# A decoder layer on one core: the FFN down projection with tokens as output rows instead of output columns

## The reference

```python
def conv_ffn(x, prev, up, cw, cb, down):
    a = x @ up
    gate, val = jnp.split(a, 2, axis=-1)
    gc, new = causal_conv(gate, prev, cw)
    h = jax.nn.gelu(gc + cb, approximate=True) * val
    return h @ down, new
...
    f, new_ffn = conv_ffn(rmsnorm(x, g_ffn_pre), ffn_prev, ffn_up, ffn_conv_w, ffn_conv_b, ffn_down)
    x = x + rmsnorm(f, g_ffn_post)
```

## Time and profile before

| | us |
|---|---|
| median of 3 runs (1368.5, 1371.78, 1371.96) | 1371.78 |
| profiled execution, span from first to last instruction | 1368.2 |
| median less span | 3.6 |
| TensorE busy (matmuls / weight loads) | 1335.9 / 1324.1 |
| VectorE, ScalarE, GpSimd busy | 759.0, 505.5, 115.1 |

### The profile page before, as it was taken

How to read it: one execution, slowest core, us unless ns; L and a number is a source line. 1 busy time by engine, 2 the same in 40 slices (tenths; PEclk the granted TensorE clock), 3 DMA queues, 4 the chain that set the end, 5 groups by cost and what they waited for, 6 DMA issues and landing times.

```text
span 1368.2 us, 24903 instructions
## 1 busy us (share of the span) xinstructions
PE 1335.9 (98%) x9043; PEld 1324.1 (97%) x9043; DVE 759.0 (55%) x1153; ACT 505.5 (37%) x731; POOL 115.1 (8%) x224
## 2 busy tenths in 40 slices
PE   6999999999989999999999999999999999999996
PEld 5999999999978999999999999999999999999995
DVE  7457755544468655544655554455554456555544
ACT  4333333333454333333333333333332333333653
POOL 4551000000034000000000000000000000000001
PEclk9999999999989999999999999999999999999998
DMA  8655455555534555456545545645545565454543
GB/s 249 162 142 135 118 147 144 150 154 149 146 110 109 143 148 153 126 149 183 143 137 154 143 128 149 190 131 157 145 134 142 152 169 157 135 154 124 138 130 97
DMA packets 383104, 199.30 MB, mean 146 GB/s; under 512 B 3924, under 2 KB 380224, under 8 KB 383064
## 3 DMA queue, kind: packets, MB, share of 16 engines
q1 hardware_dynamic: 382992, 198.56, 52.9%
q0 software_dynamic: 80, 0.31, 0.1%
HBM read 195.42 MB, written 3.56 MB: 145 GB/s over the span
## 4 chain that ended last, share of the span: by engine, by line
PE 94%; DVE 2%; SPq 2%; POOL 1%; DMA 1%; issue 0%; ACT 0%; DVEq 0%; ACTq 0%
PE mm L438 30%; PE mm L442 30%; PE mm L439 30%; POOL xT L1438 1%; DMA raw<-in_w_in_dram 1%; SPq L309 1%; PE tb L688 1%; DVE y_tok L1340 1%; DVE w_lo L948 1%; PE tb L480 0%; PE tb L438 0%; DVE sq L1227 0%; PE tb L439 0%; PE tb L442 0%; SPq L323 0%
## 5 line engine op out<-in xcount | busy, mean ns | idle before, releaser
L438 PE MATMUL mm<-a_hi,w_hi 128*128 128x320 f32 x1888 | 588.3, 312 | 0.4 <-DVE w_lo L948 0.4
L442 PE MATMUL mm<-a_lo,w_hi 128*128 128x320 f32 x1888 | 586.2, 310 | 1.9 <-DVE a_lo L1003 1.8
L439 PE MATMUL mm<-a_hi,w_lo 128*128 128x320 f32 x1888 | 585.3, 310 | 0.0
L718 ACT ACTIVATE w_hi<-raw 128x1024 fp32r (+3 forms) x404 | 370.7, 966 | 456.4 <-PE mm L442 444.9
L948 DVE TENSOR_TENSOR w_lo<-raw,w_hi 128x1024 fp32r<-128x1024 f32 (+1 forms) x404 | 441.8, 1135 | 133.3 <-ACT w_hi L718 133.3
L442 PEld LDWEIGHTS mm<-a_lo,w_hi 128*128 128x128 f32 x1888 | 355.3, 188 | 3.7 <-DVE a_lo L1003 3.6
L438 PEld LDWEIGHTS mm<-a_hi,w_hi 128*128 128x128 f32 x1888 | 355.3, 188 | 1.7 <-DVE w_lo L948 0.7
L439 PEld LDWEIGHTS mm<-a_hi,w_lo 128*128 128x128 f32 x1888 | 355.3, 188 | 0.3
L438 PE MATMUL mm<-m_hi,w_hi 128*128 128x320 f32 x960 | 299.2, 312 | 0.0
L442 PE MATMUL mm<-m_lo,w_hi 128*128 128x320 f32 x960 | 297.3, 310 | 0.0
L439 PE MATMUL mm<-m_hi,w_lo 128*128 128x320 f32 x960 | 297.3, 310 | 0.0
(11 more groups left out here) (184 smaller groups left out, 666.5 us busy)
## 6 DMA issues: line engine op xcount, KB each, us to landing
raw<-in_ffn_up_dram SPq DMA_DIRECT2D x88, 1024.0 KB, 5.7
raw<-in_ffn_down_dram SPq DMA_DIRECT2D x64, 704.0 KB, 4.8
raw<-in_w_in_dram SPq DMA_DIRECT2D x34, 1024.0 KB, 5.6
raw<-in_w_out_dram SPq DMA_DIRECT2D x16, 1024.0 KB, 6.0
x_tok<-in_x_prompt_dram SPq DMA_DIRECT2D x4, 512.0 KB, 6.9
out_dram<-y_tok SPq DMA_DIRECT2D x8, 256.0 KB
x_tok<-in_x_sample_dram SPq DMA_DIRECT2D x4, 128.0 KB, 6.8
out_dram<-y_tok SPq DMA_DIRECT2D x4, 128.0 KB
```

Of the source, the lines that this page charges most:

```text
L438: pe.matmul(out, w_hi[:, s], tile(hi, k), start=start, stop=False)
L439: pe.matmul(out, w_lo[:, s], tile(hi, k), start=False, stop=False)
L442: return pe.matmul(out, w_hi[:, s], tile(lo, k), start=False, stop=stop)
L718: act.activation(w_hi[:, d:d + half], src, ACT.Copy).then_inc(w_hi_done, 1)
```

## The change

The down projection of each group is computed the other way round: a block of `h` (128 inner channels, up to 128 tokens) is the stationary operand and 512 columns of `ffn_down` move past it, so that a result has tokens as rows and 512 output channels along the free side.

- **Pieces.** A group has 4 column quarters `n`, each in three weight pieces `j` of 4, 4 and 3 inner blocks (`PARTS`), 12 pieces in all (`N_PIECES`), each 512 columns wide. Per inner block and quarter TensorE does `down_row` for the three token tiles in the order `D_TILES` = (2, 0, 1): three matmuls for each full tile, two for the sample tile. For the samples `h_hi` holds the 64 rounded columns and beside them the 64 columns of what is left, so one 128-wide stationary operand does both with w_hi, the result's halves being added up at the end; w_lo takes a stationary operand of 64 columns. That is 8 matmuls of 512 columns where before there were 4 x 3 = 12 of 320, and 4 x 4 x 11 x 8 = 1408 in all.
- **Banks.** The sums are in the six `tb` banks, three for each of two quarters in turn. VectorE adds them to `f_tok` (`add_rows`, `sum_rows`), which lies where `f` was. The `mm` banks are free for the units.
- **End.** No unit turns `f`, and `token_sums(4)` is gone. ScalarE squares each row piece and sums it along the row in the same instruction (`square_row`). The gain comes as a row spread over the partitions by one transfer from ScalarE's queue; GpSimd multiplies the first three quarters by it, VectorE the last (`gain_last`). In the last group the last two pieces are interleaved by token tile, so that the tiles end one after the other, and each has its own factor. Twelve pieces leave: seven on VectorE (`leave`), five on ScalarE and GpSimd.
- **Elsewhere.** GpSimd's zeroing of `f` is gone, the second part of `h` is made by two VectorE instructions instead of one, and some small regions change place.

```diff
-    PER_GROUP = 2 * NG + KD
+    QD = D // 512
+    PARTS = [(0, 4), (4, 4), (8, NG - 8)]
+    N_PIECES = len(PARTS) * QD
+    PER_GROUP = 2 * NG + N_PIECES
+    D_TILES = (2, 0, 1)
...
+    f_tok = sb("f_tok", [P, QD, 3, 512], where="f")
+    gain = sb("gain", [P, D], where="a_hi", plus=24576)
+    s_low = sb("s_low", [TS, 512], where="a_hi", plus=24576 + 8192)
+    junk = sb("junk", [P, 512], where="acc")
+    h_hi = sb("h_hi", [P, NG, HW], F32R, where="m_hi")
+    h_lo = sb("h_lo", [P, NG, SEQ], F32R, where="m_lo")
+    ssq = sb("ssq", [P, 3, QD])
...
-        UNITS = sorted([(m, "x", m // 3, m % 3) for m in range(3 * (KD // 4))] +
-                       [(4 * k4 + 5 + i, "f", k4, i) for k4 in range(KD // 4 - 1) for i in range(3)] +
-                       [(12, "state", n, 0) for n in range(2)])
-        UNITS += [(KD, "f", KD // 4 - 1, i) for i in range(3)]
-        Y_POOL = [(1, 0), (1, 2), (2, 2)]
-        Y_ORDER = [(k4, i) for k4 in range(QD) for i in range(3) if (k4, i) not in Y_POOL]
+        UNITS = [("x", n // 3, n % 3) for n in range(3 * QD)] + [("state", n, 0) for n in range(2)]
+        UNIT_AT = {6 + n: n for n in range(len(UNITS))}
+        N_UNITS = len(UNITS)
+
+
+        Y_POOL = [(0, 2), (1, 2), (0, 0), (1, 0), (0, 1)]
+        Y_ORDER = [(2, 2), (3, 2), (2, 0), (3, 0), (1, 1), (2, 1), (3, 1)]
 
...
+                for j in range(N_PIECES):
+                    n, (k0, nk) = j // len(PARTS), PARTS[j % len(PARTS)]
+                    load(C_FFN // 2 + g * (PER_GROUP // 2) + NG + j // 2, j % 2,
+                         down[:, bass.ds(g * NG + k0, nk), n * 512:(n + 1) * 512], 4 * nk, 512)
...
+            def down_row(g, e, i, k, slot, start, stop, bank):
+
+                t0, nt = TT[i]
+                o = (e * 4 + slot) * 512
+                whi, wlo = w_hi[:, o:o + 512], w_lo[:, o:o + 512]
+                hi = h_hi[:, k, t0:t0 + nt]
+                if nt == P:
+                    pe.matmul(bank[:, :], hi, whi, start=start, stop=False)
+                    pe.matmul(bank[:, :], hi, wlo, start=False, stop=False)
+                    return pe.matmul(bank[:, :], h_lo[:, k, t0:t0 + nt], whi,
+                                     start=False, stop=stop)
+                both = h_hi[:, k, t0:t0 + 2 * nt]
+                if start:
+                    pe.matmul(bank[:, :], both, whi, start=True, stop=False)
+                    return pe.matmul(bank[0:nt, :], hi, wlo, start=False, stop=stop)
+                pe.matmul(bank[0:nt, :], hi, wlo, start=False, stop=False)
+                return pe.matmul(bank[:, :], both, whi, start=False, stop=stop)
+
...
+            def piece_ready(g, j):
+                pe.wait_ge(w_lo_done, 2 * (C_FFN + g * PER_GROUP + 2 * NG + j) + 2)
+
+            def down_tile(g, j, x):
+
+                n, (k0, nk) = j // len(PARTS), PARTS[j % len(PARTS)]
+                i = D_TILES[x]
+                if k0 == 0:
+                    if type(g) is int and g == GROUPS - 1 and n >= 2:
+                        pe.wait_ge(full_done, 3 * (n - 2) + x + 1)
+                    elif type(g) is not int or 4 * g + n >= 2:
+                        pe.wait_ge(rows_taken, 3 * (QD * g + n - 2) + x + 1)
+                for k in range(k0, k0 + nk):
+                    if n == 0 and x == 0:
+                        ready_h(g, k)
+                    last = down_row(g, j % 2, i, k, k - k0, k == 0, k == NG - 1, tb[3 * (n % 2) + x])
+                return last
+
+            def down_piece(g, j, beside=None):
+                piece_ready(g, j)
+                for x in range(3):
+                    last = down_tile(g, j, x)
+                    if x == 2:
+                        last.then_inc(used, 1)
+                    elif j % len(PARTS) == len(PARTS) - 1:
+                        last.then_inc(rows_done, 1)
+                    if beside and x < 2:
+                        beside(2 * j + x)
+
+            def down_pieces(g):
+                for j in range(N_PIECES):
+                    down_piece(g, j)
...
-            for m in range(KD):
-                mine = [n for n, u in enumerate(UNITS) if u[0] == m]
-                chunk(C_FFN // 2 + g * (PER_GROUP // 2) + NG + m // 2, m % 2, m_hi, m_lo, range(NG),
-                      ready_h(h_hi_done, g), ready_h(h_lo_done, g),
-                      {3 + 2 * x: [lambda n=n: turn_unit(n)] for x, n in enumerate(mine)})
-            token_sums(4)
-            for n, u in enumerate(UNITS):
-                if u[0] == KD:
-                    turn_unit(n)
+            for j in range(N_PIECES - 2):
+                down_piece(g, j, beside)
+            j = N_PIECES - 2
+            piece_ready(g, j)
+            piece_ready(g, j + 1)
+            for x in range(3):
+                down_tile(g, j, x)
+                down_tile(g, j + 1, x).then_inc(used if x == 2 else rows_done, 1)
...
+            def split_piece(g, j):
+
+                blocks = KD if j >= N_PIECES else 4 * PARTS[j % len(PARTS)][1]
+                split_hi(C_FFN // 2 + g * (PER_GROUP // 2) + NG + j // 2, j % 2, blocks)
+
+            def down_splits(g):
+                for j in range(N_PIECES):
+                    split_piece(g, j + 2)
...
+            def square_row(n, x):
+
+                i = D_TILES[x]
+                nt = TT[i][1]
+                act.wait_ge(full_done, 3 * n + x + 1)
+                act.wait_ge(row_squared, 3 * n + x)
+                act.activation(junk[0:nt, :], f_tok[0:nt, n, i, :], ACT.Square,
+                               accum_out=ssq[0:nt, i, n:n + 1]).then_inc(row_squared, 1)
...
+            act.preload_act_table(ACT.Sqrt)
+            for j in range(N_PIECES):
+                for x in range(2):
+                    if 2 * j + x in UNIT_AT:
+                        take_unit(UNIT_AT[2 * j + x])
+                if j < N_PIECES - 2:
+                    split_piece(GROUPS - 1, j + 2)
+                if j == 0:
+                    act.dma_start(gain[:, :], g_ffn_post.to_broadcast([P, D])).then_inc(gain_b_in, 16)
+                if j % len(PARTS) == 0 and j:
+                    for x in range(3):
+                        square_row(j // len(PARTS) - 1, x)
+            for x in range(3):
+                square_row(QD - 1, x)
+                root_of(x)
+                if x == 0:
+                    scale_row(0, 0)
+                    scale_row(0, 1)
+                elif x == 1:
+                    scale_row(1, 2)
+                    scale_row(1, 3)
+            scale_row(2, 4)
...
-                dve.tensor_tensor(tile(m_lo, i), val[:, :], tile(m_hi, i).bitcast(F32),
+                dve.tensor_tensor(h_tile(h_lo, SEQ, i, 0, SEQ), val[:, 0:SEQ],
+                                  h_tile(h_hi, HW, i, 0, SEQ).bitcast(F32), ALU.subtract)
+                dve.tensor_tensor(h_tile(h_hi, HW, i, T, HW), val[:, SEQ:T],
+                                  h_tile(h_hi, HW, i, SEQ, T).bitcast(F32),
                                   ALU.subtract).then_inc(h_lo_done, 1)
...
+            def add_rows(g, n, x):
+
+                i, bank = D_TILES[x], tb[3 * (n % 2) + x]
+                wait_rows(g, n, x)
+                mine = f_tok[:, n, i, :]
+                if type(g) is int and g == 0:
+                    dve.tensor_copy(mine, bank[:, :]).then_inc(rows_taken, 1)
+                else:
+                    dve.tensor_tensor(mine, bank[:, :], mine, ALU.add).then_inc(rows_taken, 1)
...
+            def sum_rows(n, x):
+
+                g, i, bank = GROUPS - 1, D_TILES[x], tb[3 * (n % 2) + x]
+                wait_rows(g, n, x)
+                if i < 2:
+                    mine = f_tok[:, n, i, :]
+                    dve.tensor_tensor(mine, bank[:, :], mine, ALU.add).then_inc(full_done, 1)
                     return
...
+                mine, other = f_tok[0:TS, n, i, :], f_tok[TS:P, n, i, :]
+                dve.tensor_tensor(s_low[:, :], bank[TS:P, :], other, ALU.add).then_inc(halves_made, 1)
+                dve.tensor_tensor(mine, bank[0:TS, :], mine, ALU.add).then_inc(halves_made, 1)
+                dve.wait_ge(halves_made, 2 * n + 2)
+                dve.tensor_tensor(mine, mine, s_low[:, :], ALU.add).then_inc(full_done, 1)
...
+            def gain_last(x):
+
+                i = D_TILES[x]
+                mine = f_tok[0:TT[i][1], QD - 1, i, :]
+                dve.tensor_tensor(mine, mine, gain[0:TT[i][1], (QD - 1) * 512:QD * 512],
+                                  ALU.mult).then_inc(gained_last, 1)
...
+            g = GROUPS - 1
+            step(dve.memset(ssq[:, :, :], 0.0))
+            for j in range(N_PIECES - 1):
+                if j % len(PARTS) == len(PARTS) - 1:
+                    for x in range(3):
+                        sum_rows(j // len(PARTS), x)
+                if j < N_PIECES - 2:
+                    split_piece(g, j + 2)
+            dve.wait_ge(row_squared, 3 * (QD - 1))
+            step(dve.tensor_reduce(rest[:, :], ssq[:, :, 0:QD - 1], mybir.AxisListType.X, ALU.add))
```

(78 more changed lines are left out.)

271 lines of the change are left out of this document (124 added, 147 removed).

## The result

The changed kernel took 1377.25 us (median of 4 runs, 1375.55 to 1379.51) beside 1370.72 us for the kernel before on the same chip (4 runs, 1368.5 to 1371.96). The ratio is 1.0053, 95% interval 1.0039 to 1.0066: half a per cent slower. The forecast was 1376.7 us. One of the later runs, of turn_twice, took 1895.5 us at a mean granted clock of 0.655 and is left out of every comparison.

What follows compares the result with a forecast made beforehand. TensorE was taken as the bound until the end work. Terms 9.4 - 3.9 + 2.9 + 1.0 - 4.5 = +4.9 us gave a 1373.1 us span, plus 3.6 for the median 1376.7 us; range 1358 to 1389.

Steps and rivals of the forecast that it cites:

- Bound by TensorE: Whole span until the end work: only TensorE's time counts, busy 98% of the span, with other engines waiting for it.
- Price of 512 columns: Down matmuls: 226.7 ns each, columns plus a fixed 13.3 ns; 1408 replacing 2112 of 320 columns, +9.4 us.
- Rival D: Sample tile: each of 352 changes between 64 and 128 stationary columns costs 0.07 us, +25 us, 1401; chance 0.04.
- a spread of the sample tile's starts: Down parts: if alternating 64 and 128 stationary columns spreads these starts, the prediction is wrong.
- Rival A: Down matmuls: the remainder hides, 213.3 ns or little more per 512 columns, -13.9 us together, 1358; chance 0.18.
- Rival C: Down matmuls: the remainder grows in proportion to columns, 234.7 ns per 512, +16 us, 1388; chance 0.16.
- Rival E: Between weight pieces elsewhere than the joint: pieces come late, up to 16 x 1 us; chance 0.02.
- Turning: Last down part: 36 transposes of f, at 109 ns each, go, -3.9 us.
- Joining: Last two pieces: joined matmuls wait for a split that starts only when piece 9 is done, +2.9 us.
- Clock: Behind the joint's wait: half clock for 3.41 us may follow, +1.0 us, between 0 and 1.6.
- The end: Behind the last matmul: 13.0 us of end work instead of 17.5, -4.5 us, give or take 1.5.
- The sum: Whole kernel: all terms together +4.9 us, 1373.1 on the profiled span, 1376.7 with 3.6 added for the median.

Runs made afterwards that it cites:

- turn_twice: Changed kernel with the transposes of nine of the twelve xT units made twice, 36 more in the last down part: 1382.31 us, ratio 1.0081.
- all_wide: Changed kernel with the sample tile's w_lo product given 128 stationary columns instead of 64, so none is narrower: 1374.32 us, ratio 1.0034.
- the probe: Separate kernel of float32r matmuls alone, 48 per shape, layer not computed, run once: 146.7 ns at 320 moving columns, 227.5 at 512, with 128 stationary.
- halves: all_wide with each 512-column matmul made as two of 256, 704 in a down part: 1393.63 us, ratio 1.0157.
- own_place: Changed kernel with the last weight piece split into SBUF that xT no longer needs, not into piece 9's place: 1372.99 us, ratio 1.0022.
- apart: Changed kernel with the last two pieces run one after the other instead of joined: 1377.67 us, ratio 1.0052.
- own_wide: Changed kernel with the edits of own_place and all_wide together: 1371.19 us, ratio 1.0008 to the kernel before.

## Why the prediction held, step by step

- **Bound by TensorE: right.** In the middle of the span nothing delays it, before or after, and the terms below that are on its path show in full.
- **Price of 512 columns: the mechanism right, the term mis-sized.** Full-width matmuls cost the 226.7 ns chosen (all_wide's 79.81 us). The term was +9.4 and measured +11.4: 4 x (79.81 - 77.44) = 9.5 for the full-width price, and 4 x 0.49 = 2.0 for the 44 matmuls a part with 64 stationary columns and what they do to their neighbours. Rival D put 0.07 us on each of 352 changes of width, 25 us in all; the 2.0 is the most that can be of its kind, since part of it is the narrow width itself. The prediction's own sign of it, a spread of the sample tile's starts, did come, but small: 231.1 ns on average instead of 226.7., cited against D, have transposes of 128 moving columns; at 320 the probe shows no cost either, only at 512.
- **Rival A fell** (the probe: no shrinking remainder from 256 to 512 columns; halves: a repeated stationary operand pays too), and so did the Trainium skill's page TensorE: Matmul & The Clock Gate (Back-to-back issue gap): 215.8 ns by it, 226.7 measured. (The page gives that gap for an isolated matmul and states a shorter sustained one, about 131 ns at 512 columns; no stretch here averages under 226.7 at 512.) **Rival C fell**: 234.7 by it. **Rival E** did not show: no gap between pieces but the joined one.
- **Turning: right**, -3.9 forecast. turn_twice puts 36 back for 3.85; by the ledger 3.5 came off. The difference of 0.4 is spread over the 14 units left, 0.03 us each, an estimate from 6.44 us for 55 transposes.
- **Joining: right.** +2.9 forecast, +3.1 measured, by own_place due to the shared place. The forecast took the joint as given; it did not ask what the joint buys. apart shows 5.1 us of the end, so nearly nothing in sum, and own_place shows that the price need not be paid.
- **Clock: right in kind, low.** +1.0 forecast of a possible 1.6; all 1.6 came, none of it hidden: the 3.41 us at 0.50 were full of matmuls.
- **The end: right**, 12.3 us for a forecast 13.0, -5.1 for -4.5. This miss and the clock's cancel.
- **The sum.** +4.9 forecast, +6.5 between the medians, +8.0 between the profiled executions (the runs of the changed kernel spread over 4.0 us, those of before over 3.5). By the ledger the terms came 2.6 too low. That the forecast of the time was off by only 0.6 us is partly luck: it added 3.6 to the span for the median, the distance of the median of before from its profiled span. In every run whose span is on record the time is 1.7 to 1.9 us over the span (the changed kernel's profiled run: 1377.92 for 1376.2), so about half of the 3.6 was that one execution being quicker than the median; with 1.7 the forecast would have been 1374.8. The median of before also fell by 1.1 with a fourth run.

What the experiments leave: the change as made costs 11.4 us of matmuls, and saves 8.6 (3.5 and 5.1); the 4.7 us of wait and slow clock made it clearly slower. Without them and the narrow operands it is about level with the kernel before (own_wide 1.0008). A mixture, three groups as before and only the last with tokens as rows, would save 3 x (79.81 - 77.44) = 7.1 us against own_wide and pay 3.9 to 5.1 for turning `f` (36 to 48 transposes); that estimate, 2 to 3 us, was not tried.

## What to carry to other kernels

Price a matmul as its columns plus a fixed start and then count both: fewer, longer matmuls lose when tiles that don't fill make more columns, here 6.7% more against a third fewer starts. When two transfers or splits are made to share a place so that work can be joined, ask what the engine does while the place is refilled; a free region elsewhere took 4.7 us off the last down part, and 4.3 off the median. Before handing elementwise work to GpSimd at the end of a kernel, look at the greatest duration of VectorE's operations beside it: here giving three outputs back to VectorE took 0.2% off the kernel before, where the whole change added 0.5%.
